# Stick-breaking attention with suffix sums in two float32r passes, one mask matmul and projection quarters between the pairs

## The chip, the cores and the metric

The kernel runs on 1 core of one Trainium2 chip. The metric is the device time in microseconds (us) of one launch, lower is better. The engines are named PE (TensorE, with its weight loads as PEld), DVE (VectorE), ACT (ScalarE), POOL (GpSimd) and SP (SyncE, which issues DMAs).

## What is computed

Two two-layer blocks run one behind the other on a sequence of 256 tokens of width 1024: gated linear attention and an MLP, differential attention and an MLP, retention and a convolutional FFN, stick-breaking attention and a convolutional FFN. The change touches the stick-breaking attention (16 heads of width 64, blocks of 128) and the boundary behind it.

```python
def _stick_breaking(h, w_in, w_out):
    q, k, v = heads(h @ w_in)                 # (B, 16, 256, 64) each
    for i in range(nb):                       # nb = 2 blocks of 128 queries
        def step(carry, xs):                  # key blocks j = i .. 0
            suffix, acc = carry
            z = jnp.einsum('bhqd,bhkd->bhqk', qb, kb) * scale
            mask = s_pos[None, :] < t_pos[:, None]
            log1m = jnp.where(mask, jax.nn.log_sigmoid(-z), 0.0)
            excl = lax.cumsum(log1m, axis=3, reverse=True) - log1m
            log_a = jax.nn.log_sigmoid(z) + excl + suffix[..., None]
            a = jnp.where(mask, jnp.exp(log_a), 0.0)
            acc = acc + jnp.einsum('bhqk,bhkd->bhqd', a, vb)
            suffix = suffix + jnp.sum(log1m, axis=3)
            return (suffix, acc), None
    return o @ w_out                          # then x = x + this
```

With z the masked scores, log1m is minus softplus(z), and the exponent of a weight is z minus the sum of softplus over this key and all later ones that the query sees. The kernel forms that sum over keys as a matmul with a triangular matrix of -1.

## The kernel before

All engines run a program written out by hand, each in its own fixed order, and meet at semaphores. Products with weights are made of three float32r matmuls: high by high, high by low and low by high. A weight chunk of 128 x 2048 is loaded by SP into one of four slots of `raw`; ACT copies its high half to `w_hi` (`hi(c)`), DVE subtracts to give `w_lo` (`lo(c)`), PE multiplies. A slot's `w_hi` may be written again when PE has used it (`used`), its `raw` when `lo` is done.

The attention treats two heads at a time, a pair p = 0..7. The scores of a pair are kept transposed (keys on partitions) in two PSUM banks, `s_bank(p)` and the next, one bank for a head, each with three blocks of 128 columns: key block 0 by query blocks 0 and 1, then key block 1 by query block 1. The steps of a pair are:

- PE `s_scores(p)` (from line 2202): float32 products of `s_k` and `s_q`, then the mask, added by float32r matmuls of the identity with the mask, one for each diagonal block (line 2214).
- ACT `s_log(p)`: ln(1 + exp(-|z|)) in three instructions (lines 958, 960, 962) into `s_b[:, p % 3, 0]`.
- DVE `s_soft(p)` (line 1599): max(z, 0) plus that, the softplus, 768 wide, into `s_b[:, p % 3, 1]`.
- PE `s_weights(p)` (lines 2224, 2226): float32 matmuls of the triangular and the all -1 matrix with these sums, added onto the scores in PSUM. `spm` is waited for.
- ACT `s_exp(p)` (line 967), then PE `s_output(p)` (lines 2237, 2239) with `s_v`, into bank 0 or 1 by turns (for pairs 6 and 7 banks 4 and 5, `so_bank`).
- ACT `s_out(p)` (line 973) copies the output's high half to `h_hi`, DVE `s_lo(p)` (line 1604) subtracts for `h_lo`.

PE's order in the loop is `s_weights(p + 1)`, `s_output(p)`, `s_scores(p + 3)`; ACT's is `s_exp(p)`, `s_out(p - 1)`, `s_log(p + 2)`; DVE's is `s_soft(p + 1)`, `s_lo(p - 1)`. Behind the loop stands the output projection with chunks C_SO to C_SO + 3, which are C_SV + 4 to C_SV + 7 of `hi` and `lo`: two chunks by `h_rows` (line 1650) and two by `last_two` (line 1682), which finishes one output bank after the other. `boundary` is then the passage to the next stage: additions to `x` (line 1117), squares, mean, POOL's power, scaling by DVE (line 1060), transposes on PE (`norm_tile`, line 1695), scaling by ACT (line 632), the split by DVE (lines 1077, 1078), and the first two chunks of the FFN (`first_two`, line 1712).

## Time and profile before

| | us |
|---|---|
| median of 3 runs | 1417.42 |
| lowest and highest | 1415.96, 1417.97 |
| the profiled execution | 1415.18 |
| its span in the trace | 1413.4 |
| PE busy | 1353.4 (96% of the span) |
| DVE busy | 953.1 (67%) |
| ACT busy | 673.1 (48%) |

The span goes from the first to the last instruction of the trace. Busy time is the time in which an engine had an instruction under way. Matmuls overlap: a duration includes the way through the array, so what a matmul costs PE is the distance from its start to the next start. A "line" is a line of the kernel, which can be that of a helper.

### The profile page before, as it was taken

The page shows a single profiled execution, that of the slowest core. Times are in us where ns is not written, and L with a number is a line of the kernel's source. Part 1 is how long each engine was busy: PE and PEld are TensorE (multiplying, and loading weights), DVE is VectorE, ACT ScalarE, POOL GpSimd, SP SyncE. Part 2 cuts the span into 40 slices and gives each one's busy share as a digit, 9 for nine tenths or more (in the row PEclk, how much of TensorE's full clock was granted, in tenths as well). Part 3 has the DMA queues.
Part 4 walks back from the last instruction along what each step waited for, and adds up shares of the span by engine and source line. Part 5 has one row for each costly group of instructions (what it writes and reads, how often), then busy time and mean ns, then how long its engine had stood idle before and what let it go on. Part 6 is the DMA issues. An engine that isn't in the chain of part 4 may idle for free.

```text
span 1413.4 us, 20048 instructions
## 1 busy us (share of the span) xinstructions
PE 1353.4 (96%) x8392; PEld 1189.1 (84%) x8392; DVE 953.1 (67%) x1197; ACT 673.1 (48%) x882; POOL 78.5 (6%) x148
## 2 busy tenths in 40 slices
PE   6899899999999899999899999999999999999997
PEld 1797799998787689998698878999998987999996
DVE  4698787776696876655784445686777534686774
ACT  1553354444556464444533454654545457654542
POOL 1111011110010200000000010000000000000000
PEclk9999999999999999999999999999999999999999
DMA  9786278786392447555265434455553531454530
GB/s 370 276 349 261 89 291 307 289 298 245 137 375 100 160 153 260 218 181 192 105 238 181 176 120 179 149 209 182 188 194 123 216 142 49 160 209 179 187 141 30
DMA packets 46105, 279.41 MB, mean 198 GB/s; under 512 B 5200, under 2 KB 5200, under 8 KB 18880
## 3 DMA queue, kind: packets, MB, share of 16 engines
q1 hardware_dynamic: 33264, 231.57, 44.3%
q0 software_dynamic: 12752, 46.57, 8.8%
q8 instruction: 66, 1.08, 0.3%
q14 instruction: 23, 0.19, 0.0%
HBM read 277.07 MB, written 1.05 MB: 197 GB/s over the span
## 4 chain that ended last, share of the span: by engine, by line
PE 85%; DVE 8%; ACT 3%; issue 2%; DMA 1%; POOL 0%; SPq 0%; POOLq 0%; DVEq 0%; ACTq 0%
PE ps L1650 33%; PE ps L1776 11%; PE ps L1778 11%; PE ps L1777 11%; PE ps L1712 4%; PE ps L1682 3%; DVE w_lo L1010 2%; DMA ada<-in_ada_w 1%; PE ps L1743 1%; PE ps L2010 1%; PE ps L1838 1%; PE ps L1811 1%; DVE acc L1022 1%; DVE h_lo L1078 1%; PE ps L2224 1%
## 5 line engine op out<-in xcount | busy, mean ns | idle before, releaser
L1010 DVE TENSOR_TENSOR w_lo<-raw,w_hi 128x2048 fp32r<-128x2048 f32 x210 | 479.7, 2290 | 178.8 <-ACT w_hi L606 178.2
L606 ACT ACTIVATE w_hi<-raw 128x2048 fp32r<-128x2048 f32 x210 | 400.4, 1911 | 202.9 <-PE ps L1650 154.6
L1776 PE MATMUL ps<-h_hi,w_hi 128*128 128x256 f32 x1344 | 381.8, 284 | 1.9 <-ACT m_r L783 1.9
L1777 PE MATMUL ps<-h_lo,w_hi 128*128 128x256 f32 x1344 | 380.3, 283 | 0.0
L1778 PE MATMUL ps<-h_hi,w_lo 128*128 128x256 f32 x1344 | 380.3, 283 | 0.0
L1776 PEld LDWEIGHTS ps<-h_hi,w_hi 128*128 128x128 f32 x1344 | 256.3, 191 | 4.1 <-ACT m_r L783 2.3
L1777 PEld LDWEIGHTS ps<-h_lo,w_hi 128*128 128x128 f32 x1344 | 256.3, 191 | 1.9 <-issue 0.2
L1778 PEld LDWEIGHTS ps<-h_hi,w_lo 128*128 128x128 f32 x1344 | 256.3, 191 | 0.0
L1561 DVE SCALAR_TENSOR_TENSOR f_cv<-ps,cols,f_cv 128x254 f32<-128x254 f32 (+1 forms) x176 | 76.7, 478 | 70.9 <-ACT f_cv L919 69.3
L1650 PE MATMUL ps<-w_hi,hid_hi 128*128 128x512 f32 x368 | 114.5, 392 | 0.0
L1650 PE MATMUL ps<-w_hi,hid_lo 128*128 128x512 f32 x368 | 114.3, 392 | 0.0
L1650 PE MATMUL ps<-w_lo,hid_hi 128*128 128x512 f32 x368 | 114.1, 391 | 0.0
L1650 PE MATMUL ps<-w_hi,h_hi 128*128 128x512 f32 x328 | 109.4, 397 | 0.4 <-issue 0.4
L1650 PE MATMUL ps<-w_lo,h_hi 128*128 128x512 f32 x328 | 107.1, 390 | 0.0
L1650 PE MATMUL ps<-w_hi,h_lo 128*128 128x512 f32 x328 | 106.9, 389 | 0.0
L1022 DVE SCALAR_TENSOR_TENSOR acc<-ada,csil,acc 128x512 f32<-128x512 f32 x146 | 99.8, 747 | 9.2 <-DMA ada<-in_ada_w 8.9
L919 ACT ACTIVATE f_cv<-ps,cols 128x256 f32<-128x256 f32 x88 | 44.8, 559 | 97.2 <-PE ps L1778 93.6
L1650 PEld LDWEIGHTS ps<-w_lo,hid_hi 128*128 128x128 f32 x368 | 69.1, 188 | 15.1
L1650 PEld LDWEIGHTS ps<-w_hi,hid_lo 128*128 128x128 f32 x368 | 69.1, 188 | 15.0
L1650 PEld LDWEIGHTS ps<-w_hi,hid_hi 128*128 128x128 f32 x368 | 66.1, 188 | 12.0 <-issue 0.5
L1650 PEld LDWEIGHTS ps<-w_hi,h_hi 128*128 128x128 f32 x328 | 61.0, 189 | 14.4 <-issue 2.1
L1650 PEld LDWEIGHTS ps<-w_lo,h_hi 128*128 128x128 f32 x328 | 61.8, 188 | 13.2 <-issue 0.2
(292 smaller groups left out, 1697.6 us busy)
## 6 DMA issues: line engine op xcount, KB each, us to landing
raw<-in_stream SPq DMA_DIRECT2D x210, 1024.0 KB, 4.8
ada<-in_ada_w POOLq DMA_DIRECT2D x80, 512.0 KB, 6.0
ada<-in_ada_w SPq DMA_DIRECT2D x8, 512.0 KB, 12.8
raw<-in_ada_w SPq DMA_DIRECT2D x8, 512.0 KB, 15.6
row<-in_gate_b POOLq DMA_DIRECT2D x3, 512.0 KB, 3.9
x<-in_x SPq DMA_DIRECT2D x1, 1024.0 KB, 9.9
retc<-in_retc POOLq DMA_DIRECT2D x1, 1024.0 KB, 4.9
out<-xn SPq DMA_DIRECT2D x2, 512.0 KB, 2.7
```

What stands on the lines that cost most here:

```text
L606: act.activation(w_hi[:, s, :], raw[:, s, :], ACT.Copy).then_inc(hi_done[s], 1)
L919: last = act.activation(f_cv[:, g % 2, value, f, :], ps[:, 4 + 2 * (g % 2) + value, f * T:(f + 1) * T], ACT.Identity, bias=cols[:, k + 3:k ...
L1010: dve.tensor_tensor(w_lo[:, s, :], raw[:, s, :], w_hi[:, s, :].bitcast(f32), ALU.subtract)\
L1022: dve.scalar_tensor_tensor(acc[:, half], rows, ck, acc[:, half], ALU.mult, ALU.add)\
L1078: dve.tensor_tensor(h_lo[:, *part], h32[:, *part], h_hi[:, *part].bitcast(f32), ALU.subtract)\
L1561: last = dve.scalar_tensor_tensor(v, src, cols[:, k:k + 1], v, ALU.mult, ALU.add)
L1650: return pe.matmul(ps[:, 2 * t + n, :], lhs, w, start=first, stop=stop and k == 1 and p == 2)
L1682: last = pe.matmul(ps[:, 2 * t + n, :], (high, high, low)[p], w, start=False, stop=second == k == 1 and p == 2)
L1712: last = pe.matmul(ps[:, 2 * t + second, 0:T], (high, high, low)[p], w, start=kt == p == 0, stop=kt == KT - 1 and p == 2)
L1776: pe.matmul(out, wh, h_hi[:, kt, :], start=kt == 0, stop=False)
L1777: pe.matmul(out, wh, h_lo[:, kt, :], start=False, stop=False)
L1778: last = pe.matmul(out, wl, h_hi[:, kt, :], start=False, stop=kt == KT - 1)
```

## The change

- Suffix sums: DVE splits the softplus sums into `s_high` (rounded to float32r) and `s_rest` (what is left), and `s_weights` runs the triangular and the -1 matrix over both in float32r. The two matrices are copied, rounded, into `maskr` at the start.
- The blocks in a bank now stand in the order key 0 by query 0, key 1 by query 1, key 0 by query 1, so that both diagonal blocks are neighbours and one mask matmul of 256 columns covers them.
- The output of every pair goes to bank 1. DVE makes both halves (`s_split`); ACT's `s_out` is gone. `s_output(p)` waits until the split of pair p - 1 is done.
- The projection is cut into 16 quarters of six matmuls (`s_project(i, t, n)`: chunk i, token tile t, column half n). Two stand between the pairs, behind p = 3 and p = 5.
- `hi(C_SV + 6)` goes ahead of ACT's last `s_exp`; the order at the boundary is written out anew, with `lo(C_F1)` and `lo(C_F1 + 1)` ahead of the first tile's split.

```diff
-        maskr = sb("maskr", [P, 4 * P], f32r)
+        maskr = sb("maskr", [P, 7 * P], f32r)
+        s_rest = at("s_rest", 6144, [3, 2, 2, 3 * P], f32r)
+        s_high = at("s_high", 10752, [2, 2, 3 * P], f32r)
 ...
+            act.activation(maskr[:, 4 * P:7 * P], shp[:, S_SBM:S_SBM + 3 * P], ACT.Copy).then_inc(mask_done, 1)
 ...
             for p in range(SH_ // 2):
                 s_exp(p)
-                if p >= 1:
-                    s_out(p - 1)
                 if p + 2 < SH_ // 2:
                     s_log(p + 2)
-            s_out(SH_ // 2 - 1)
-            hi(C_SV + 6)
+                if p == 6:
+                    hi(C_SV + 6)
             hi(C_SV + 7)
 ...
             def s_soft(p):
                 dve.wait_ge(sln, p + 1)
-                if p >= 3:
-                    dve.wait_ge(e_mm, p - 2)
-                dve.scalar_tensor_tensor(s_b[:, p % 3, 1, :, :], ..., ALU.max, ALU.add).then_inc(spm, 1)
-
-            def s_lo(p):
+                if p >= 2:
+                    dve.wait_ge(e_mm, p - 1)
+                sums = s_b[:, p % 3, 1, :, :]
+                link(dve.scalar_tensor_tensor(sums, ..., ALU.max, ALU.add))
+                link(dve.tensor_copy(s_high[:, p % 2, :, :], sums))
+                dve.tensor_tensor(s_rest[:, p % 3, 1, :, :], sums, s_high[:, p % 2, :, :].bitcast(f32), ALU.subtract)\
+                    .then_inc(spm, 1)
+
+            def s_split(p):
+                dve.wait_ge(so_mm, p + 1)
+                dve.tensor_copy(h_hi[:, p, :], ps[:, 1, 0:T]).then_inc(so_hi, 1)
                 dve.wait_ge(so_hi, p + 1)
-                dve.tensor_tensor(h_lo[:, p, :], ps[:, so_bank(p), 0:T], h_hi[:, p, :].bitcast(f32), ALU.subtract)\
+                dve.tensor_tensor(h_lo[:, p, :], ps[:, 1, 0:T], h_hi[:, p, :].bitcast(f32), ALU.subtract)\
                     .then_inc(so_lo, 1)
 ...
-                for f, b in half:
-                    for first in (0, T):
-                        last = pe.matmul(ps[:, b, first:first + P], maskr[:, 0:P], maskr[:, 3 * P:4 * P], ...)
+                for f, b in half:
+                    last = pe.matmul(ps[:, b, 0:2 * P], maskr[:, 0:P], maskr[:, 3 * P:5 * P], ...)
 ...
             def s_weights(p):
                 pe.wait_ge(spm, p + 1)
                 for i in range(2):
-                    sums, b = s_b[:, p % 3, 1, i, :], s_bank(p) + i
-                    pe.matmul(ps[:, b, 0:3 * P], shp[:, S_NU:S_NU + P], sums, ...)
-                    last = pe.matmul(ps[:, b, P:2 * P], shp[:, S_NO:S_NO + P], sums[:, 2 * P:3 * P], ...)
+                    b = s_bank(p) + i
+                    for sums in (s_high[:, p % 2, i, :], s_rest[:, p % 3, 1, i, :]):
+                        pe.matmul(ps[:, b, 0:3 * P], maskr[:, 5 * P:6 * P], sums, ...)
+                        last = pe.matmul(ps[:, b, 2 * P:3 * P], maskr[:, 6 * P:7 * P], sums[:, P:2 * P], ...)
                 last.then_inc(e_mm, 1)
 ...
                 pe.wait_ge(sexp, p + 1)
-                if p >= 2:
-                    pe.wait_ge(so_lo, p - 1)
+                if p:
+                    pe.wait_ge(so_lo, p)
 ...
+            def s_project(i, t, n):
+                s = chunk_ready(C_SO + i) if t == n == 0 else (C_SO + i) % NSLOT
+                if t == n == 0:
+                    pe.wait_ge(so_lo, 2 * i + 2)
+                if i == 0 and (t, n) == (0, 1):
+                    pe.wait_ge(so_lo, 8)
+                for k in range(2):
+                    high, low = h_pair(2 * (i // 2))(i % 2, k, t)
+                    for p in range(3):
+                        w = (w_hi, w_lo, w_hi)[p][:, s, k * D + n * 512:k * D + (n + 1) * 512]
+                        last = pe.matmul(ps[:, 2 * t + n, :], (high, high, low)[p], w, ...)
 ...
                 if p + 3 < SH_ // 2:
                     s_scores(p + 3)
-            pe.wait_ge(so_lo, 6)
-            for i in range(2):
-                h_rows(C_SO + i, i, 4)
-            last_two(C_SO + 2, C_SO + 3, h_pair(2), (so_lo, 8), lambda: norm_tile(7, 0))
+                if p in (3, 5):
+                    s_project((p - 3) // 2, 0, 0)
+            s_project(2, 0, 0)
+            s_project(3, 0, 0)
+            for i in range(4):
+                s_project(i, 0, 1)
+            for i in range(4):
+                s_project(i, 1, 0)
+                s_project(i, 1, 1)
+                if i == 2:
+                    norm_tile(7, 0)
```

Two places in the order of the instructions. First PE, from the weights of one pair to the weights of the next. In the kernel before (L2224 and L2226 are the weights, L2237 and L2239 the output, L2208, L2210 and L2214 the scores and masks):

```order
L2224 MATMUL ps<-s_b,shp 128x384 [waits spm]
L2226 MATMUL ps<-s_b,shp 128x128
L2224 MATMUL ps<-s_b,shp 128x384
L2226 MATMUL ps<-s_b,shp 128x128
L2237 MATMUL ps<-s_b,s_v 64x256 [waits so_lo,sexp]
L2237 MATMUL ps<-s_b,s_v 64x256
L2239 MATMUL ps<-s_b,s_v 64x128 x2
L2208 MATMUL ps<-s_q,s_k 128x256 [waits sexp]
L2208 MATMUL ps<-s_q,s_k 128x256
L2210 MATMUL ps<-s_q,s_k 128x128 x2
L2214 MATMUL ps<-maskr 128x128 x4
L2224 MATMUL ps<-s_b,shp 128x384 [waits spm]
```

Weights, output, scores, masks of the pair stand directly behind one another, with nothing of the projection among them. In the changed kernel the same pair, followed by the first quarter of the projection (L2282):

```order
L2250 MATMUL ps<-s_high,maskr 128x384
L2252 MATMUL ps<-s_high,maskr 128x128
L2250 MATMUL ps<-s_rest,maskr 128x384
L2252 MATMUL ps<-s_rest,maskr 128x128
L2263 MATMUL ps<-s_b,s_v 64x256 [waits so_lo,sexp]
L2263 MATMUL ps<-s_b,s_v 64x256
L2266 MATMUL ps<-s_b,s_v 64x128 x2
L2233 MATMUL ps<-s_q,s_k 128x2x128 [waits sexp]
L2233 MATMUL ps<-s_q,s_k 128x2x128
L2236 MATMUL ps<-s_q,s_k 128x128 x2
L2239 MATMUL ps<-maskr 128x256 x2
L2282 MATMUL ps<-w_hi,h_hi 128x512 [waits so_lo,lo_done1,hi_done1]
```

The weights are eight matmuls in two passes instead of four in one, the masks two instead of four, and the quarter stands between the scores and the next pair's weights.

Second DVE, from the last two pairs to the first addition to `x`. Before (L1599 is the softplus sum, L1604 the output's low half, L1010 a chunk's low half, L1117 an addition to `x`):

```order
L1599 SCALAR_TENSOR_TENSOR s_b<-ps,s_b 128x768 [waits e_mm,sln]
L1604 TENSOR_TENSOR h_lo<-ps,h_hi 128x256 [waits so_hi]
L1599 SCALAR_TENSOR_TENSOR s_b<-ps,s_b 128x768 [waits e_mm,sln]
L1604 TENSOR_TENSOR h_lo<-ps,h_hi 128x256 [waits so_hi] x3
L1010 TENSOR_TENSOR w_lo<-raw,w_hi 128x2048 [waits hi_done3]
L1010 TENSOR_TENSOR w_lo<-raw,w_hi 128x2048 [waits hi_done0]
L1010 TENSOR_TENSOR w_lo<-raw,w_hi 128x2048 [waits hi_done1]
L1010 TENSOR_TENSOR w_lo<-raw,w_hi 128x2048 [waits hi_done2]
L1117 TENSOR_TENSOR x<-x,ps 128x512 [waits y_part] x2
```

The last three low halves of outputs follow one another, and all four chunks of this stretch (slots 3, 0, 1 and 2) come ahead of the additions. The same place in the changed kernel (L1604, L1606 and L1607 are the sum and its split, L1612 and L1614 the output's, L1014 a chunk's low half, L1121 an addition):

```order
L1604 SCALAR_TENSOR_TENSOR s_b<-ps,s_b 128x768 [waits e_mm,sln]
L1606 CAST s_high<-s_b 128x768 [waits dve_chain]
L1607 TENSOR_TENSOR s_rest<-s_b,s_high 128x768 [waits dve_chain]
L1612 CAST h_hi<-ps 128x256 [waits so_mm]
L1614 TENSOR_TENSOR h_lo<-ps,h_hi 128x256 [waits so_hi]
L1612 CAST h_hi<-ps 128x256 [waits so_mm]
L1614 TENSOR_TENSOR h_lo<-ps,h_hi 128x256 [waits so_hi]
L1014 TENSOR_TENSOR w_lo<-raw,w_hi 128x2048 [waits hi_done3]
L1612 CAST h_hi<-ps 128x256 [waits so_mm]
L1614 TENSOR_TENSOR h_lo<-ps,h_hi 128x256 [waits so_hi]
L1014 TENSOR_TENSOR w_lo<-raw,w_hi 128x2048 [waits hi_done0]
L1121 TENSOR_TENSOR x<-x,ps 128x512 [waits y_part] x2
```

Each sum has become three instructions, each output's low half two, and the low half of slot 3 (chunk C_SO + 2) stands between the last two splits. The low halves of slots 1 and 2 (C_F1 and C_F1 + 1) have moved behind the first two additions.

## Rows read from the trace of the kernel before

**Rows 1.** Busy time by stretch: from:to, length, PE, PEld, DVE, ACT, POOL, PEclk, DMA, GB/s.

```profile
1151.49:1190.74 39.25, 38.00 (x249) 27.78 (x248) 10.63 (x15) 30.48 (x43) 0.00 (x0) 1.00 0.07 27
1190.74:1213.50 22.76, 22.76 (x106) 18.82 (x105) 13.18 (x13) 11.56 (x18) 0.55 (x1) 1.00 0.49 185
1240.00:1260.00 20.00, 20.00 (x134) 18.46 (x134) 18.57 (x27) 11.43 (x12) 0.00 (x0) 1.00 0.72 263
```

**Rows 2.** Timeline of PE, one pair: start, length, engine, line, operation, count, idle before.

```profile
1167.01 0.86 PE L2224 MATMUL ps<-s_b,shp 128*128 128x384 f32 x2
...
1168.89 0.65 PE L2237 MATMUL ps<-s_b,s_v 128*64 128x256 f32 x4
...
1169.69 0.70 PE L2208 MATMUL ps<-s_q,s_k 64*128 64x256 f32 x4
...
1170.55 0.66 PE L2214 MATMUL ps<-maskr 128*128 128x128 f32 x4
1171.05 0.86 PE L2224 MATMUL ps<-s_b,shp 128*128 128x384 f32 x2
```

**Rows 3.** Timeline of ACT, the same pair: abs (L958) and exp of the weights (L967).

```profile
1167.21 0.81 ACT L958 ACTIVATE s_b<-ps 128x768 f32<-128x768 f32 x1 [0.41 <-PE ps L2214]
...
1169.77 0.79 ACT L967 ACTIVATE s_b<-ps 128x768 f32<-128x768 f32 x1
...
1171.24 0.81 ACT L958 ACTIVATE s_b<-ps 128x768 f32<-128x768 f32 x1 [0.41 <-PE ps L2214]
```

**Rows 4.** Timeline of DVE, the sum of the same pair.

```profile
1169.90 0.96 DVE L1599 SCALAR_TENSOR_TENSOR s_b<-ps,s_b 128x768 f32<-128x768 f32 x1 [2.64 <-ACT s_b L962]
```

**Rows 5.** Timeline of PE: end of the value projection, last weights, start of the output projection.

```profile
1159.80 0.81 PE L2224 MATMUL ps<-s_b,shp 128*128 128x384 f32 x2
...
1187.04 0.91 PE L2224 MATMUL ps<-s_b,shp 128*128 128x384 f32 x2 [1.15 <-DVE s_b L1599]
...
1190.74 0.73 PE L1650 MATMUL ps<-w_hi,h_hi 128*128 128x512 f32 x2
```

**Rows 6.** Timeline of PE in the differential attention: its masks, then the next product.

```profile
437.76 0.51 PE L2037 MATMUL ps<-maskr 128*128 128x256 f32 x2
438.10 0.40 PE L2010 MATMUL ps<-w_hi,h_hi 128*128 128x512 f32 x1
```

**Rows 7.** Groups of DVE by form: line, operation, shapes, count, busy, mean ns, idle before.

```profile
L1077 DVE CAST h_hi<-h 128x256 fp32r<-128x256 f32 x56 | 16.3, 291 | 19.9 <-ACT h L632 19.9
...
L1579 DVE TENSOR_TENSOR hid_lo<-f_p,hid_hi 128x512 fp32r<-128x512 f32 x22 | 15.2, 692 | 0.8
...
L1578 DVE CAST hid_hi<-f_p 128x512 fp32r<-128x512 f32 x22 | 9.4, 427 | 1.9 <-PE ps L1650 1.2
...
L1272 DVE COPY g_st<-ps 128x256 f32<-128x256 f32 x4 | 1.7, 420 | 0.9 <-PE ps L1913 0.9
```

**Rows 8.** The page's costliest groups: the low and the high half of a chunk.

```profile
L1010 DVE TENSOR_TENSOR w_lo<-raw,w_hi 128x2048 fp32r<-128x2048 f32 x210 | 479.7, 2290 | 178.8 <-ACT w_hi L606 178.2
L606 ACT ACTIVATE w_hi<-raw 128x2048 fp32r<-128x2048 f32 x210 | 400.4, 1911 | 202.9 <-PE ps L1650 154.6
```

**Rows 9.** Timeline of DVE: the fourth addition to x behind the projection.

```profile
1214.59 0.68 DVE L1117 TENSOR_TENSOR x<-x,ps 128x512 f32<-128x512 f32 x1
```

**Rows 10.** Timeline of PE: the second tile's transposes and the product behind them.

```profile
1217.88 1.03 PE L1695 MATMUL ps<-shp,xn 128*128 128x128 f32 x8
1218.67 0.36 PE L1712 MATMUL ps<-w_hi,h_hi 128*128 128x256 f32 x1
```

**Rows 11.** Busy time by stretch, as in rows 1, where PE worked little.

```profile
458.00:464.00 6.00, 2.99 (x25) 2.43 (x23) 5.89 (x14) 4.05 (x23) 2.89 (x7) 1.00 0.11 15
464.00:470.00 6.00, 3.60 (x20) 3.41 (x21) 5.56 (x20) 1.06 (x6) 1.94 (x4) 0.69 0.40 162
470.00:476.00 6.00, 4.91 (x29) 4.42 (x28) 2.66 (x8) 4.06 (x19) 2.69 (x6) 0.74 0.00 0
680.00:700.00 20.00, 13.82 (x78) 11.25 (x76) 15.58 (x31) 9.92 (x26) 2.32 (x3) 1.00 0.16 58
```

More of the change, by code:

```diff
@@ L718, in _ @@
             act.activation(maskr[:, 0:P], ident, ACT.Copy)
-            act.activation(maskr[:, P:4 * P], shp[:, S_CAUS:S_CAUS + 3 * P], ACT.Copy).then_inc(mask_done, 1)
+            act.activation(maskr[:, P:4 * P], shp[:, S_CAUS:S_CAUS + 3 * P], ACT.Copy)
+            act.activation(maskr[:, 4 * P:7 * P], shp[:, S_SBM:S_SBM + 3 * P], ACT.Copy).then_inc(mask_done, 1)
             act.wait_ge(ada_pe, KT)
@@ L968, in s_exp @@
                     .then_inc(sexp, 1)
-            def s_out(p):
-                act.wait_ge(so_mm, p + 1)
-                act.activation(h_hi[:, p, :], ps[:, so_bank(p), 0:T], ACT.Copy).then_inc(so_hi, 1)
             s_log(0)
@@ L979, in _ @@
                 s_exp(p)
-                if p >= 1:
-                    s_out(p - 1)
                 if p + 2 < SH_ // 2:
                     s_log(p + 2)
-            s_out(SH_ // 2 - 1)
-            hi(C_SV + 6)
+                if p == 6:
+                    hi(C_SV + 6)
             hi(C_SV + 7)
+            scale_col = lambda kt: cols[:, COL_FFN + KT + kt:COL_FFN + KT + kt + 1]
+            square(X_SB, 0)
+            square(X_SB, 1)
             hi(C_F1)
             hi(C_F1 + 1)
-            boundary(7, X_SB, TR_N7, lambda kt: cols[:, COL_FFN + KT + kt:COL_FFN + KT + kt + 1], None, C_F1, 5)
+            norm_tile(TR_N7, 0, scale_col, None)
+            square(X_SB, 2)
+            square(X_SB, 3)
+            hi(C_F1 + 2)
+            evacuate(5, 0, (fc_mm, 11), ACT.Copy)
+            norm_tile(TR_N7, 1, scale_col, None)
+            evacuate(5, 1, (fc_mm, 12), ACT.Copy)
+            hi(C_F1 + 3)
+            evacuate(5, 2, multiplied(C_F1), ACT.Copy)
+            evacuate(5, 3, multiplied(C_F1 + 1), ACT.Copy)
             ffn(1, C_F1)
@@ L1611, in _ @@
                 if p >= 1:
-                    s_lo(p - 1)
-            s_lo(SH_ // 2 - 1)
+                    s_split(p - 1)
             lo(C_SV + 6)
+            s_split(SH_ // 2 - 1)
             lo(C_SV + 7)
-            for c in range(C_SO, C_SO + 2):
-                lo(c + 4)
-            boundary(add_plain, Y_SOUT, 7, TR_N7, C_F1)
+            add_plain(Y_SOUT, 0)
+            add_plain(Y_SOUT, 1)
+            norm_mean(7, 0)
+            scale_tile(7, 0)
+            lo(C_F1)
+            lo(C_F1 + 1)
+            split_tile(TR_N7, 0, 0, 4)
+            add_plain(Y_SOUT, 2)
+            add_plain(Y_SOUT, 3)
+            norm_mean(7, 1)
+            scale_tile(7, 1)
+            split_tile(TR_N7, 1, 0, 4)
+            lo(C_F1 + 2)
+            lo(C_F1 + 3)
             ffn(1, C_F1)
```

36 lines of the change are left out of this document (22 added, 14 removed).

## The prediction

> **What bounds the kernel now.** I read busy time by stretch first [rows 1], then the instructions of one pair of heads in order of time on PE, ACT and DVE [rows 2 to 4]. The change touches one stage, from the first scores at 1151.49 us to the end of the output projection at 1213.5 us: 62 of 1413.4 us. In it PE is busy 38.00 of 39.25 us over the eight pairs and all 22.76 us of the projection [rows 1], so PE sets the pace. The reader should see in [rows 2] that a pair costs 4.04 us of PE: weights 1167.01 to 1168.89 = 1.88, output to 1169.69 = 0.80, scores with masks to 1171.05 = 1.36 (masks alone 1170.55 to 1171.05 = 0.50).
>
> A second limit lies close behind. The scores of a pair must pass ACT (abs, exp, ln), DVE (the softplus sum) and come back to PE for the weights, and two pairs are in flight. Around that loop: abs starts 1167.21, DVE's sum ends 1170.86, PE could start at 1170.91: 3.70 us [rows 3, 4]. Then PE's 1.88 + 0.80 + 1.36, then 0.20 from the scores' end at 1171.05 to the next abs at 1171.24. Together 7.94 us for two pairs, against 8.06 of PE work. The slack is 0.12 us for two pairs. That is the number on which this forecast hangs: whatever shortens PE by more than it gives nothing, and whatever lengthens ACT or DVE inside the loop is paid.
>
> **The masks.** Four 128-column float32r matmuls become two of 256 columns. The first form takes 0.50 us [rows 2], the second stands in the earlier attention at 437.76 to 438.10 = 0.34 [rows 6]. Scores fall from 1.36 to 1.20. The strided output of the scores has no row. Its ends are 0 and, if each half paid a start of its own, 0.10 a pair. I take 0.
>
> **The weights.** Per pair, four matmuls of plain float32 (two of 384 and two of 128 columns, each two records) become eight of float32r. The projection's 96 matmuls of 512 columns, six to a quarter, take (22.76 - 0.79) / 96 = 0.229 us each [rows 1, 10]; 0.79 is a tile's transposes (1217.88 to 1218.67). At the full clock a column is 1/2.4 ns, so 384 columns take 0.229 - 0.053 = 0.175. A 128-column one follows from the two mask forms: 4x - 2 x 0.122 = 0.50 - 0.34, x = 0.10. Weights then cost 4 x 0.175 + 4 x 0.10 + 0.12 for the change of type = 1.22 us, against 1.88. Ends: 1.06 (128 columns at the column rate) and 1.35 (0.125 each, 0.15 for the change). I take 1.22, which has the nearest row.
> The Trainium skill (TensorE: Matmul & The Clock Gate, section Back-to-back issue gap) gives an isolated gap of N/2.4 + 2.5 ns, 56 ns at 128 columns. By it the weights would cost about 1.04 and the end would come near 1419.8; the mask rows speak for 0.10 and the row decides.
>
> **PE in sum.** 0.16 + 0.66 = 0.82 us less per pair, 6.6 us over eight. PE needs 3.22 us a pair.
>
> **The split of the sums (DVE).** To feed float32r, DVE casts the 768-wide sum to s_high and subtracts it to give s_rest, both before the weights may start. A cast takes 0.291 at 256 and 0.427 at 512 [rows 7], so 0.565 at 768. A subtraction takes 0.692 at 512 and 2.290 at 2048 [rows 7, 8], so 0.958. Each waits some 0.04 for the instruction before it. That adds 1.60 us inside the loop. Ends: 1.45, and 2.0 if the cast ran at the subtraction's rate.
>
> **The loop after.** 3.70 + 1.60 + 1.22 + 0.80 + 1.20 + 0.20 = 8.72 us for two pairs, 4.36 a pair, where it was 4.03. The 6.6 us taken from PE become idle time, and each pair is 0.33 us longer than before. The quarters of the projection go into that idle time (4.36 - 3.22 = 1.14), but one quarter is 1.37.
>
> **The copy of the output.** The h_hi copy moves from ACT to DVE, where a 256-wide copy from PSUM takes 0.420 [rows 7]. With the subtraction a split is 0.89. All outputs now share bank 1, so output(p) waits for split(p-1). Within the loop DVE has that time free. At the end it has not: output(7) stands right behind output(6), with no work between.
>
> **The walk.** Two shorter scores bring the value projection's end from 1159.80 [rows 5] to 1159.48. Weights(0) and scores(2) end at 1161.90, abs at 1162.10, and weights(2) start at 1167.40 (before: 1167.01). The odd chain: scores(3) end 1165.12, ACT is free at 1165.35, weights(3) at 1170.75 with 0.1 for a split ahead on DVE. Weights(4) at 1176.12; PE is through with scores(6) at 1179.34 and then does the first quarter until 1180.71, while weights(5) could have started at 1179.47. So that quarter pushes the odd chain by 1.24. Weights(6) at 1184.84, the second quarter (1186.86 to 1188.23) is hidden, weights(7) at 1180.71 + 3.42 + 5.30 = 1189.43. Before it was 1187.04 [rows 5]. Output(6) ends 1191.45, split(6) is done at 1192.5, output(7) ends 1193.35. Before: 1190.74 [rows 5]. ACT's high half of C_SO+2, moved ahead of exp(7), fits in ACT's wait and costs nothing.
>
> **The projection.** Two quarters are done, 14 are left. The low half of chunk C_SO+2 stands on DVE behind split(6): 1192.5 + 2.29 = 1194.8 [rows 8]. PE waits 1.5 us for it. Then split(7), and the low half of C_SO+3 until 1197.9: PE waits 1.7 us again. Before, both chunks were long ready. The fourth quarter ends at 1199.3, twelve more 16.4, the transposes 0.79: end at 1216.5, against 1213.5. The two waits, 3.2 us, eat the 2.7 us that the quarters between the pairs had won. **+3.0 us.**
>
> **The next boundary.** Before, DVE's fourth addition to x starts at 1214.59, 1.05 us behind the projection's end, and the second tile's transposes start 3.29 later at 1217.88 [rows 9, 10]. Now both additions of tile 1 stand behind the low halves of C_F1 and C_F1+1 and the splits of tile 0. PE frees C_F1+1's slot 2.7 us before the transposes of tile 0; high half 1.91 and low half 2.29 [rows 8] then end 1.8 us before the projection's end, the splits 0.9 behind it, and the fourth addition starts 1.5 behind it. PE waits some 0.3 us longer. **+0.3 us.** ffn(1) behind it is bound by PE (20.00 of 20.00, [rows 1]), so the shift goes through to the end. The wider mask copy at the kernel's start is one ACT instruction where ACT has nothing to do: 0.
>
> **Sum.** +3.3 us: the profiled span of 1413.4 becomes 1416.7, its own time of 1415.18 becomes 1418.5. The median shown is 1417.42, 2.2 us above that execution, so 1417.42 + 3.3 = **1420.7 us**, 0.23% slower. About 0.2%, 2.8 us, is what a measurement can tell from no change, and my sum lies close to that line. Moving one term at a time through the walk: weights at 1.06 takes off 0.8, at 1.35 adds 0.65; the split at its high end adds 1.2; a strided output at 0.10 adds 0.5. Terms together span about +1.3 to +5.5.
>
> **Rivals.**
> *A, as summed*: 1420.7, own range 1420.2 to 1422.5. Chance 0.45.
> *B, the cheap ends*: weights near 1.06, the PSUM copy at the SBUF cast's 0.29, and a shorter split. The same mechanism gives +1.5 to +2.7, near 1419.5, no measurable change. For it speaks that the 128-column cost rests on a difference of two rows. 0.33.
> *C, PE's clock falls*. From 1188.2 to 1198 PE works in my walk some 4.4 of 9.8 us. In the earlier attention PE was busy 2.99 of 6 us from 458 to 464, and the granted clock was 0.69 and 0.74 over the two stretches behind it, so it stood at 1.2 GHz for about 6.8 us [rows 11]. In a stretch bound by PE that costs about half, 3.4 us: 1424.1. Against it: from 680 to 700 us PE was busy 13.82 of 20 us and the clock stayed 1.00 [rows 11], and no single wait in my walk exceeds 1.8 us. 0.13.
> The Trainium skill (TensorE: Matmul & The Clock Gate, section What's actually happening) says that the throttled clock is the default and activity releases it; both rows fit that, and neither tells how thin 1188 to 1198 may be.
> *D, the other side: the loop does not bind*. If ACT already held each pair's scores when it got free, pairs would be spaced by what each engine does: DVE 2.56 + 0.81 = 3.4, ACT 3.3, PE 3.22 and the quarters. Weights(7) would start near 1186.3, 3.1 us sooner than in my walk: 1417.6, not slower. It decides as soon as scores(p+3) end before exp(p+1) does; in [rows 2, 3] they end after it with today's order, which the change keeps. 0.05. With B's costs on top, or without the two waits for low halves, it is faster by more than 0.2% (about 1414.5): 0.04.
>
> Slower 0.58, same 0.38, faster 0.04. The range, 1417.5 to 1424.3, takes in A, B, most of D and half of C.
>
> **What would show it.** In the changed kernel's trace: weights blocks of about 1.2 us spaced by some 4.4 us, PE idle 1.1 us before most of them, released by DVE's s_rest; weights(7) near 1189.4; two PE waits of 1.5 and 1.7 us for w_lo at the third and fourth quarter; the end of the projection near 1216.5. Wrong if pairs are 3.4 us apart, if the cast takes 0.96, or if the granted clock drops near 1195.

## The result and the profile after

| | before | after |
|---|---|---|
| median | 1416.7 us (5 runs, 1415.5 to 1417.97) | 1422.27 us (5 runs, 1421.14 to 1424.66) |
| ratio | | 1.0042, 95% interval [1.0029, 1.0055] |
| the profiled execution, its span | 1415.18, 1413.4 | 1421.14, 1419.4 |
| PE, DVE, ACT busy | 1353.4, 953.1, 673.1 | 1352.8, 967.8, 671.5 |

The changed kernel is 0.4% slower. PE's busy time is the same to 0.6 us although its matmuls got cheaper. Stages ahead of this one take a different time in each execution (the first scores start at 1151.49 us before, at 1150.65 after, and between 1151.95 and 1153.78 in the profiled executions of the experiments), so I compare the stretch from the first scores to the second tile's transposes of the next boundary. It was 1217.88 - 1151.49 = 66.39 us [rows 10] and is 1223.81 - 1150.65 = 73.16 us: **6.77 us longer**.

First PE's time line of the changed kernel (start, duration, engine, line, operation; in brackets the idle time ahead and its releaser), which answers to [rows 2] and [rows 6]. L2250 and L2252 are the weights, L2263 and L2266 the output, L2233 and L2236 the scores, L2239 the mask:

```profile
1160.99 0.34 PE L2250 MATMUL ps<-s_high,maskr 128*128 128x384 f32 x1
1161.16 0.22 PE L2252 MATMUL ps<-s_high,maskr 128*128 128x128 f32 x1
1161.23 0.39 PE L2250 MATMUL ps<-s_rest,maskr 128*128 128x384 f32 x1
1161.45 0.22 PE L2252 MATMUL ps<-s_rest,maskr 128*128 128x128 f32 x1
1161.51 0.39 PE L2250 MATMUL ps<-s_high,maskr 128*128 128x384 f32 x1
...
1162.18 0.65 PE L2263 MATMUL ps<-s_b,s_v 128*64 128x256 f32 x4
...
1162.98 0.70 PE L2233 MATMUL ps<-s_q,s_k 64*128 64x256 f32 x4
...
1163.83 0.50 PE L2239 MATMUL ps<-maskr 128*128 128x256 f32 x2
1166.48 0.44 PE L2250 MATMUL ps<-s_high,maskr 128*128 128x384 f32 x1 [2.15 <-DVE s_rest L1607]
```

Weights take 1162.18 - 1160.99 = 1.19 us (1.88 before), output 0.80, scores with masks about 1.19 (1.36 before). Then PE waits 2.15 us for DVE's `s_rest`. DVE's time line shows what it waits for, beside [rows 4]:

```profile
1163.88 0.96 DVE L1604 SCALAR_TENSOR_TENSOR s_b<-ps,s_b 128x768 f32<-128x768 f32 x1 [4.04 <-ACT s_b L961]
1164.87 0.56 DVE L1606 CAST s_high<-s_b 128x768 fp32r<-128x768 f32 x1
1165.46 0.96 DVE L1607 TENSOR_TENSOR s_rest<-s_b,s_high 128x768 fp32r<-128x768 f32 x1
1166.34 0.42 DVE L1612 CAST h_hi<-ps 128x256 fp32r<-128x256 f32 x1
```

The cast and the subtraction stand between the sum and the weights, 1.58 us. The rest is in three stretches of the changed kernel (length, then busy time and instructions of PE, PEld, DVE, ACT, POOL, granted clock, DMA share, GB/s): the pairs, the passage to the projection, and the projection, beside [rows 1]:

```profile
1150.65:1191.50 40.85, 35.02 (x231) 27.65 (x232) 24.27 (x36) 29.52 (x36) 0.00 (x0) 0.96 0.07 26
1191.50:1199.00 7.50, 4.43 (x24) 2.82 (x24) 6.01 (x6) 2.61 (x2) 0.00 (x0) 0.82 0.34 107
1199.00:1221.00 22.00, 22.00 (x100) 18.28 (x100) 10.22 (x16) 7.66 (x15) 0.55 (x1) 0.91 0.38 143
```

Before, PE was busy 38.00 of 39.25 us in the pairs and all of the projection, at clock 1.00. Now it idles 5.8 us in the pairs, 3.1 in the passage, and the granted clock is 0.96, 0.82 and 0.91. Its waits from 1191 us on:

```profile
1193.39 0.65 PE L2263 MATMUL ps<-s_b,s_v 128*64 128x256 f32 x4 [1.08 <-DVE h_lo L1614]
1195.54 0.47 PE L2282 MATMUL ps<-w_hi,h_hi 128*128 128x512 f32 x1 [1.28 <-issue]
1198.53 0.77 PE L2282 MATMUL ps<-w_hi,h_hi 128*128 128x512 f32 x1 [0.70 <-issue]
...
1223.81 1.09 PE L1716 MATMUL ps<-shp,xn 128*128 128x128 f32 x8 [0.34 <-DVE xn L1064]
```

Output(7) waits for the split of output(6) (the shared bank 1), and the third and fourth projection quarter start when DVE's low halves are through: "issue" names no releaser, but DVE's `w_lo` ends at 1193.16 + 2.28 = 1195.44 and 1196.15 + 2.28 = 1198.43, 0.1 us ahead of each. The clock in half-microsecond windows (length, PE busy, clock, DMA share, GB/s):

```profile
1175.50:1176.00 0.50, 0.50 (x5) 0.77 0.00 0
1176.00:1176.50 0.50, 0.50 (x5) 0.50 0.00 0
...
1178.50:1179.00 0.50, 0.50 (x4) 0.50 0.00 0
1179.00:1179.50 0.50, 0.50 (x6) 0.82 0.00 0
...
1196.00:1196.50 0.50, 0.50 (x4) 0.74 0.85 98
1196.50:1197.00 0.50, 0.50 (x3) 0.50 0.83 131
...
1202.50:1203.00 0.50, 0.50 (x3) 0.50 0.06 17
1203.00:1203.50 0.50, 0.50 (x4) 0.93 0.00 0
```

PE ran at 1.2 GHz from about 1175.8 to 1179.2 us (3.4 us) and from 1196.2 to 1203.0 us (6.8 us). The first fall comes behind a wait of 2.08 us ahead of weights(4), the second inside the passage, in which PE had been busy 2.34 of the 4.70 us from 1191.5 us on.

This execution is the fastest of the five. Each execution lists the mean granted clock of its whole run, and the slower it was, the lower that clock: 0.988 at 1421.14 us, 0.987 at 1421.50, 0.984 at 1422.27, 0.983 at 1424.50 and 0.982 at 1424.66. So the falls seem to be longer or more frequent in the others, of which there is no trace.

### The profile page after: what moved, and what is told of

It is laid out like the page before. It is cut to its first block, busy times and chain, and to the rows that moved or that the text cites. A ratio compares the mean times of both kernels' runs of the same rounds, so it can differ in the third digit from the quotient of the medians.

```text
span 1419.4 us, 20035 instructions
## 1 busy us (share of the span) xinstructions
PE 1352.8 (95%) x8376; PEld 1189.8 (84%) x8376; DVE 967.8 (68%) x1221; ACT 671.5 (47%) x875; POOL 78.5 (6%) x148
## 4 chain that ended last, share of the span: by engine, by line
PE 83%; DVE 9%; ACT 3%; issue 2%; DMA 1%; POOL 0%; SPq 0%; POOLq 0%; DVEq 0%; ACTq 0%
PE ps L1671 32%; PE ps L1797 11%; PE ps L1799 11%; PE ps L1798 11%; PE ps L1733 4%; PE ps L1703 2%; DVE w_lo L1014 2%; DMA ada<-in_ada_w 1%; PE ps L2282 1%; PE ps L1764 1%; PE ps L2031 1%; PE ps L1859 1%; PE ps L1832 1%; DVE acc L1026 1%; ACT w_hi L604 1%
## 5 line engine op out<-in xcount | busy, mean ns | idle before, releaser
L1014 DVE TENSOR_TENSOR w_lo<-raw,w_hi 128x2048 fp32r<-128x2048 f32 x210 | 479.8, 2290 | 175.1 <-ACT w_hi L604 174.5
L1671 PE MATMUL ps<-w_hi,h_hi 128*128 128x512 f32 x312 | 104.3, 397 | 0.3 <-issue 0.3
L1671 PE MATMUL ps<-w_lo,h_hi 128*128 128x512 f32 x312 | 102.4, 391 | 0.0
L1671 PE MATMUL ps<-w_hi,h_lo 128*128 128x512 f32 x312 | 102.0, 389 | 0.0
L1671 PEld LDWEIGHTS ps<-w_lo,h_hi 128*128 128x128 f32 x312 | 58.9, 189 | 12.6 <-issue 0.2
L1671 PEld LDWEIGHTS ps<-w_hi,h_hi 128*128 128x128 f32 x312 | 58.0, 189 | 13.6 <-issue 2.0
```

The source lines that it names most:

```text
L1014: dve.tensor_tensor(w_lo[:, s, :], raw[:, s, :], w_hi[:, s, :].bitcast(f32), ALU.subtract)\
L1671: return pe.matmul(ps[:, 2 * t + n, :], lhs, w, start=first, stop=stop and k == 1 and p == 2)
```

## The experiments

The theory: the loop of two pairs is bound by its latency (the time that a pair needs to go round PE, ACT and DVE), so cheaper PE work gives nothing and DVE's 1.6 us are paid; the quarters' gain is lost to waits for low halves at the end; the idle PE then loses its clock. The rivals are told with each run. All medians and ratios stand in this table, with the stretch from the first scores to the second transposes in each kernel's one profiled execution, the start of weights(7) behind the first scores, and the time that PE stood at 1.2 GHz in the stretch.

| kernel | ratio to before, interval | stretch | weights(7) | at 1.2 GHz |
|---|---|---|---|---|
| before | | 66.39 | 35.55 | 0 |
| after | 1.0042 [1.0029, 1.0055] | 73.16 | 39.50 | 3.4 + 6.8 |
| e1_fill | 1.0019 [1.0010, 1.0029] | 69.50 | 37.95 | 0 |
| e2_float32_sums | 1.0011 [1.0001, 1.0020] | 68.00 | 35.95 | 0 |
| e3_low_half_early | 1.0028 [1.0016, 1.0039] | 71.52 | 41.04 | 3.4 + 3.4 |
| e4_masks_alone | 0.9990 [0.9980, 0.9999] | 65.19 | 34.35 | 0 |
| e5_scores_ahead | 1.0019 [1.0009, 1.0028] | 69.40 | 35.70 | 6.8 |
| e6_masks_and_passes | 1.0036 [1.0022, 1.0049] | 70.18 | 38.45 | 3.4 + 6.8 |
| e7_ahead_before_tail | 0.9994 [0.9985, 1.0002] | 64.51 | 34.31 | 0 |
| e8_high_early | 0.9975 [0.9965, 0.9984] | 62.78 | 32.17 | 0 |
| e9_two_quarters | 0.9963 [0.9949, 0.9977] | 60.35 | 32.98 | 0 |
| e10_boundary_order | 0.9983 [0.9974, 0.9992] | 63.98 | 32.98 | 3.4 |
| e11_own_banks | 1.0047 [1.0032, 1.0063] | 71.42 | 39.48 | 3.4 + 3.4 |
| e12_banks_and_halves | 1.0019 [1.0009, 1.0029] | 68.48 | 40.65 | 6.8 |

**The clock.** The changed kernel, with matmuls on banks that nobody reads in the places where PE waits:

```diff
+            def fill(n, bank):
+                for _ in range(n):
+                    pe.matmul(ps[:, bank, 0:T], maskr[:, 0:P], maskr[:, P:3 * P], start=True, stop=True)
...
+                if p in (0, 2):
+                    fill(14, 0)
...
             s_project(2, 0, 0)
+            fill(8, 2)
```

(Seven more stand ahead of output(7), five behind the second quarter and eight ahead of the third. The edit adds 56 matmuls in all; the 42 of the expectation is a miscount.)

> The changed kernel plus 42 matmuls of 256 columns into a PSUM bank that nobody reads, put where PE stood idle in the changed kernel's trace (14 ahead of weights(2), 14 ahead of weights(4), 5 ahead of weights(7), 7 ahead of output(7), 8 ahead of each of the third and fourth quarters less the one already counted; each group shorter than the idle time). They compute nothing. Theory 1 (the fall of PE's clock is about 3.6 of the 6 us that the change costs): the granted clock stays 1.00 from the first scores to the end of the projection, that stretch takes 65.0 us instead of 68.6, and the kernel is 3 to 4 us faster than the changed one: 1418.5, ratio to before near 1.0015. Theory 2 (the pairs and the waits cost it all, the clock's fall lies in time in which PE would have waited anyway): clock 1.00 but the stretch stays at 68 us and the time at 1422 or above.

Median 1419.13 us. The clock stayed at 1.00 over the pairs, the passage and the projection:

```profile
1152.48:1193.33 40.85, 39.01 (x276) 31.94 (x276) 24.85 (x38) 31.05 (x38) 0.00 (x0) 1.00 0.07 26
1193.33:1200.00 6.67, 6.06 (x38) 4.84 (x37) 5.36 (x5) 1.11 (x1) 0.00 (x0) 1.00 0.47 160
1200.00:1221.00 21.00, 21.00 (x112) 18.03 (x112) 10.74 (x17) 9.49 (x19) 0.97 (x2) 1.00 0.38 150
```

The stretch is 69.50 us: the two falls cost 3.66 us in the profiled execution, 1.55 ahead of weights(7) (39.50 - 37.95) and 2.11 behind it. The medians come out near it: 1422.27 - 1419.13 = 3.1.

**The passes.** One plain float32 pass in place of the two, with the rest of the change kept:

```diff
-                link(dve.scalar_tensor_tensor(sums, ...))
-                link(dve.tensor_copy(s_high[:, p % 2, :, :], sums))
-                dve.tensor_tensor(s_rest[...], sums, s_high[...].bitcast(f32), ALU.subtract).then_inc(spm, 1)
+                dve.scalar_tensor_tensor(s_b[:, p % 3, 1, :, :], ...).then_inc(spm, 1)
```

> The changed kernel with the suffix sums in one float32 pass again (no s_high, no s_rest); block order, one mask matmul, bank 1, quarters and boundary as changed. Theory 1 (DVE's split lies inside the loop of two pairs and lengthens it): weights blocks are 1.88 us and pairs 3.9 us apart, PE is hardly idle between pairs, the clock stays 1.00 there; weights(7) start 36.9 us behind the first scores (35.55 before the change, 39.5 in the changed kernel; two quarters of 1.37 are in it); the two waits for low halves remain. 1416.5 to 1418. Theory 2 (the two passes are worth their PE time and something else in the change costs, such as the shared bank or the split on DVE): as slow as the changed kernel or slower, 1422 to 1425, pairs 4.3 us or more apart.

Stretch 68.00 us, median 1417.76, clock 1.00. Weights(7) start at 35.95, 0.95 us sooner than expected. At the full clock the two passes therefore cost 69.50 - 68.00 = 1.5 us in this surrounding, and the rest of the change is 1.6 us behind the kernel before.

**The masks.** The kernel before with the block order and the one mask matmul, nothing else:

```diff
-                    for first in (0, T):
-                        last = pe.matmul(ps[:, b, first:first + P], maskr[:, 0:P], maskr[:, 3 * P:4 * P],
+                    last = pe.matmul(ps[:, b, 0:2 * P], maskr[:, 0:P], maskr[:, 3 * P:5 * P],
```

> The kernel before the change with one part of it alone: the new order of the blocks and one mask matmul of 256 columns for both diagonal blocks. Theory 1 (PE bound with a slack of 0.12 us for two pairs): a block of scores takes 1.20 instead of 1.36 us, pairs are 3.89 us apart instead of 4.03, the projection starts 1.2 to 1.5 us sooner: 1415.4, ratio 0.9991. If the strided output of the scores costs something, a block of scores takes 1.3 us or more and the gain is under 0.6 us.

Stretch 65.19, 1.20 us shorter than before; the strided output costs nothing that shows. So the part of the change beside masks and passes (one output bank, quarters, waits at the end, boundary) costs 68.00 - 65.19 = 2.8 us. It adds up from rows: two quarters leave the end (-2.74), weights(7) start 35.95 - 34.35 = 1.60 later, output(7) comes 0.88 later behind them, the third and fourth quarter wait 1.28 + 1.37, the boundary 0.1: together 2.5. The other 0.3 us I can't put down to a row.

**The low halves.** The changed kernel with the high and low half of chunk C_SO + 2 one to two pairs earlier:

```diff
+                if p == 4:
+                    hi(C_SV + 6)
                 if p + 2 < SH_ // 2:
                     s_log(p + 2)
-                if p == 6:
-                    hi(C_SV + 6)
...
                     s_split(p - 1)
+                if p == 4:
+                    lo(C_SV + 6)
```

> The changed kernel with the high half of chunk C_SO+2 made by ACT behind exp(4) and its low half by DVE behind the split of pair 3, where both engines stood idle for over 2 us. Theory 1 (PE's two waits at the end come from low halves that stand between the last splits): the wait of 1.28 us ahead of the third quarter goes, the fourth quarter's low half is ready about 2.2 us earlier, and the projection's end comes 2 to 3 us sooner if the clock's fall moves with it, at least 1.3 if it does not: 1419.5 to 1421. Theory 2 (PE has to wait for the output's last split anyway): less than 0.7 us.

The wait ahead of the third quarter is gone; the fourth waits 1.63 us, since its low half still stands behind split(7). But in this execution the clock fell twice in the pairs, behind 2.15-us waits, and not at the end:

```profile
1168.50:1169.00 0.50, 0.50 (x3) 0.50 0.00 0
...
1178.50:1179.00 0.50, 0.50 (x3) 0.66 0.00 0
```

With different falls in the two traces the 1.6 us between them can't be put down to the low half alone. Behind weights(7) the clock held both here and in e1_fill, so that part can be compared: 71.52 - 41.04 = 30.48 us here and 69.50 - 37.95 = 31.55 there. The early low half is worth 1.1 us, a little less than the 1.3 expected, since 1.28 us of waiting went and the fourth quarter's wait grew from 1.37 to 1.63.

**The shared bank.** Outputs 6 and 7 in banks 4 and 5:

```diff
+        def so_bank(p):
+            return p - 2 if p >= 6 else 1
...
-                if p:
+                if 0 < p < 6:
                     pe.wait_ge(so_lo, p)
```

> The changed kernel with outputs 6 and 7 in banks 4 and 5 and not in bank 1, so that output(7) does not wait for DVE's split of output(6). Theory: the 1.08 us wait ahead of output(7) goes, and the wait ahead of the third quarter grows by as much, since DVE's order (split, low half, split, low half) is untouched and the low half comes last: first scores to second transposes 73.1 us as in the changed kernel, 1422 us, ratio 1.004. Rival (the shared bank costs its wait): 1.1 us less, 1421.1, ratio 1.0033.

The wait ahead of output(7) is gone and stands, whole, ahead of the third quarter:

```profile
1193.70 0.65 PE L2267 MATMUL ps<-s_b,s_v 128*64 128x256 f32 x4
...
1196.83 0.47 PE L2286 MATMUL ps<-w_hi,h_hi 128*128 128x512 f32 x1 [2.26 <-issue]
...
1199.82 0.77 PE L2286 MATMUL ps<-w_hi,h_hi 128*128 128x512 f32 x1 [0.48 <-issue]
```

Third quarter at 1196.83 - 1151.95 = 44.88 us behind the first scores, in the changed kernel 1195.54 - 1150.65 = 44.89. The bank costs nothing, because DVE's order ahead of the quarters is the later limit. The trace is 1.74 us shorter all the same: its second fall lasted 3.4 us and not 6.8. The median says no such thing (1421.74 us, 1.0047), which shows how far one trace can be trusted where falls differ.

**Bank and both halves.** As the last one, with both chunks' halves made in the idle time between the pairs:

```diff
+                if p == 4:
+                    hi(C_SV + 6)
...
+                if p == 5:
+                    hi(C_SV + 7)
...
+                if p == 4:
+                    lo(C_SV + 6)
+                if p == 6:
+                    lo(C_SV + 7)
```

> As e11_own_banks, and ACT and DVE make the high and low halves of both C_SO+2 and C_SO+3 in their idle time between the pairs (behind log(6) and log(7); behind the splits of pairs 3 and 5). Theory: no wait is left between weights(7) and the transposes of the first tile, 1.0 + 1.3 + 0.7 us go, and with them the thin stretch behind which the clock fell at the end; the falls behind the 2-us waits in the pairs stay. First scores to second transposes 66.6 us at full clock, 68.1 to 70 with falls in the pairs: 1417 to 1419 us, ratio 1.0005 to 1.002. Rival (the end is limited otherwise): 71.5 or more, ratio 1.003.

No wait is left between weights(7) and the transposes of tile 0, and there is no fall at the end; one of 6.8 us remains in the pairs, behind the wait ahead of weights(2). Stretch 68.48, median 1418.73: 2.94 us less than with own banks alone, for 2.26 + 0.48 = 2.74 us of waits taken away at about as much time at 1.2 GHz.

**Latency or work.** The changed kernel, with the scores one turn earlier. Each engine does the same work.

```diff
                 s_output(p)
-                if p + 3 < SH_ // 2:
-                    s_scores(p + 3)
+                if p == 0:
+                    s_scores(3)
+                if p + 4 < SH_ // 2:
+                    s_scores(p + 4)
```

> The changed kernel with one edit: PE issues the scores of a pair one turn earlier (scores(p+4) behind output(p), where it was scores(p+3)); same instructions, same work. Theory (the latency of the loop sets the pace, because ACT must wait for scores that PE issues too late): ACT then always has the next pair's scores, and the loop of two pairs is weights to exp 1.29, exp 0.69, abs/exp/ln 2.65, the sum, cast and subtraction 2.68 = 7.31 us, 3.66 a pair, where it is 8.72. weights(7) starts 3.3 us sooner than in a run at full clock, at about 34.6 us behind the first scores (39.5 in the changed kernel), the waits ahead of the weights are under 1 us each, and the clock stays at 1.00 in the pairs. First scores to second transposes: 66.2 us if the clock also holds at the end (1416.0 us, ratio 0.9999), 68.3 if it falls there again (1418.1, 1.0013). Rival (PE or DVE work sets the pace, 4.3 us a pair): spacing stays near 4.3, ratio 1.002 to 1.004.

Weights(2), (4) and (6) start at 1169.17, 1176.74 and 1184.30: 7.57 us for two pairs, where the changed kernel has 8.77 (1166.48 to 1175.25). So order and latency set the pace there, and not an engine's work. The spacing decides this; the ratio, 1.0019, lies near the range that the rival had. The waits ahead of the weights are short:

```profile
PE ps L2250 <- DVE s_rest L1607: 2.7, 4, 1.0
PE ps L2282 <- issue: 2.0, 2, 1.3
PE ps L2263 <- DVE h_lo L1614: 1.1, 1, 1.1
```

(us in total, times, the longest.) My 7.31 was too low in two terms: from weights to exp it is 1.40 and not 1.29, from exp to abs 0.87 and not 0.69. Weights(7) start at 35.70, not 34.6. The end of the stage is the changed kernel's, and there the clock fell again, for 6.8 us:

```profile
1192.00:1194.00 2.00, 0.87 (x8) 1.00 0.00 0
1194.00:1196.00 2.00, 1.55 (x5) 0.80 0.23 37
1196.00:1198.00 2.00, 1.28 (x3) 0.50 0.94 385
```

From weights(7) to the second transposes it takes 33.70 us, in the changed kernel 33.66, in e1_fill 31.55.

**The passes in the old surroundings.** Before, with the masks and the two passes:

```diff
-                    sums, b = s_b[:, p % 3, 1, i, :], s_bank(p) + i
+                    b = s_bank(p) + i
+                    for sums in (s_high[:, p % 2, i, :], s_rest[:, p % 3, 1, i, :]):
```

> The kernel before with the one mask matmul and the two float32r passes, and nothing else of the change: outputs alternate between two banks, ACT makes their high half, the projection and the boundary stand behind the pairs as before. Theory: the loop of two pairs is as in the changed kernel, 8.7 us, so the weights start in turns of two 8.7 us apart, weights(7) near 36.6 us behind the first scores (34.35 with the masks alone), and the shorter last weights give 0.7 back: first scores to second transposes 66.8 us (65.19 with the masks alone, 66.39 before), 1416.6 us, ratio 1.0003, if the clock holds. If the 2-us waits ahead of every other weights bring it down once more, as in the changed kernel, 1.5 to 3.7 us are on top: up to 1420.3, 1.003. Rival (the passes cost nothing by themselves, the rest of the change does): 1414.3 to 1415, ratio 0.999.

Weights(2) to weights(4) 8.77 us again. The clock fell behind weights(4) and weights(6), for 3.4 and 6.8 us, and the stretch is 70.18: 5.0 us behind the masks alone. The median, 1420.58 us, lies just above the 1420.3 that I had allowed for falls. The passes, through the loop and the clock (as long at 1.2 GHz as in the changed kernel), make 5.0 of the 8.0 us by which the changed kernel's stretch is behind that of the masks alone; the projection's order isn't needed for them.

**Scores ahead, old end of the stage**, both halves of an output on DVE:

```diff
-                act.activation(h_hi[:, p, :], ps[:, so_bank(p), 0:T], ACT.Copy).then_inc(so_hi, 1)
+                dve.tensor_copy(h_hi[:, p, :], ps[:, so_bank(p), 0:T]).then_inc(so_hi, 1)
```

> The kernel of e6_masks_and_passes with the scores one turn earlier and both halves of the output split on DVE (copy and subtraction, as in the changed kernel). Theory: 3.66 us a pair, limited by ACT and DVE in turn; weights(7) at about 33.7 us behind the first scores (35.55 before, 34.35 with masks alone), last weights 1.2 us; first scores to second transposes 63.9 us, 1413.7 us, ratio 0.9983, clock 1.00. Rival (what cost 2.8 us in the changed kernel beside the passes is the split on DVE, not the order of the projection): 1416 or more, ratio 1.000.

Stretch 64.51, not 63.9, since two pairs take 7.56 here too. The median is 1415.11 us (0.9994), so no difference to before that these runs show, and 1.4 us above my forecast. It lies between the theory's time and the rival's. 5.7 us of e6's stretch are gone with the order and the copy on DVE, which no run separates, and the clock held, although PE waited 2.04 us ahead of weights(6) and 1.20 ahead of weights(7) a pair later.

**High parts first.** PE multiplies both heads' high parts while DVE still subtracts:

```diff
-                link(dve.tensor_copy(s_high[:, p % 2, :, :], sums))
+                dve.tensor_copy(s_high[:, p % 2, :, :], sums).then_inc(s_hi, 1)
+                dve.wait_ge(s_hi, p + 1)
...
-                pe.wait_ge(spm, p + 1)
-                for i in range(2):
+                for n in range(2):
+                    pe.wait_ge(spm if n else s_hi, p + 1)
+                    for i in range(2):
```

> The kernel of e7_ahead_before_tail, in which PE multiplies both heads' high parts while DVE still makes the low ones (a semaphore of its own behind the cast). Theory: 0.6 us leave the loop of two pairs (6.7 us), but DVE's own work of 3.45 us a pair (sum, cast, subtraction, split) then sets the pace: weights(7) at about 32.5 us behind the first scores, first scores to second transposes 62.7 us, 1412.5 us, ratio 0.9974. Rival (changing between high and low of the two heads costs as much as it hides, or DVE already sets the pace): as e7_ahead_before_tail, 0.998.

Stretch 62.78 for 62.7, median 1412.9 us. It beats the kernel before by 0.25%. The pace seems to be not DVE's, as I had said, but ACT's, which has nearly no gap left (from 1168 to 1182 us ACT was busy 13.31 of 14 us, DVE 12.88, PE 12.59): weights(2) to weights(4) are 6.99 us, and ACT's exponentials of pairs 3 to 5 stand as follows, 6.99 us from the first to the third:

```profile
1172.91 0.79 ACT L971 ACTIVATE s_b<-ps 128x768 f32<-128x768 f32 x1
...
1176.47 0.81 ACT L971 ACTIVATE s_b<-ps 128x768 f32<-128x768 f32 x1
...
1179.90 0.79 ACT L971 ACTIVATE s_b<-ps 128x768 f32<-128x768 f32 x1
```

**Two quarters that nothing waits for.**

```diff
-            return p - 2 if p >= 6 else p % 2
+            return p - 2 if p >= 6 else 1 if p >= 4 else p % 2
...
+                if p in (4, 5):
+                    s_project(p - 4, 0, 0)
```

> The kernel of e8_high_early with two of the sixteen projection quarters moved between the pairs, behind output(4) and output(5), where PE waits about 1.0 us for s_high; outputs 4 and 5 share bank 1 so that bank 0 is free for them, outputs 6 and 7 keep banks of their own, and the rest of the projection and the boundary stay as before. Theory (a quarter between the pairs wins what it fills, if nothing behind it comes to wait for a low half or a bank): 2.74 us of projection leave the end, the last weights start some 1.0 us later: first scores to second transposes 61.1 us (62.78 in e8_high_early, 66.39 before), 1411.2 us, ratio 0.9963, clock 1.00. Rival (the quarters are what costs in the changed kernel): 62.8 or more, ratio 0.9975 or above.

Stretch 60.35 us, **1410.1 us median, 0.9963**: faster than both kernels. The quarters are worth 62.78 - 60.35 = 2.4 us here: weights(7) start only 0.8 later, 2.74 leave the end, and the last weights take 1.19 us and not 1.71, because `s_rest` is ready in time. The quarters fill nearly all that PE had left to wait ahead of the weights:

```profile
1152.42:1189.00 36.58, 35.68 (x248) 28.19 (x248) 25.62 (x40) 30.21 (x37) 0.00 (x0) 1.00 0.08 29
```

**The boundary's order.** The last kernel with the changed kernel's order on ACT and DVE behind the projection:

```diff
-            for c in range(C_SO, C_SO + 2):
-                lo(c + 4)
-            boundary(add_plain, Y_SOUT, 7, TR_N7, C_F1)
+            add_plain(Y_SOUT, 0)
...
+            scale_tile(7, 0)
+            lo(C_F1)
+            lo(C_F1 + 1)
+            split_tile(TR_N7, 0, 0, 4)
+            add_plain(Y_SOUT, 2)
```

> The kernel of e9_two_quarters with the changed kernel's order at the next boundary (DVE: both additions of tile 1 behind the low halves of C_F1, C_F1+1 and the splits of tile 0). Theory, as forecast: PE starts the second tile's transposes about 0.3 us later: 61.4 us against 61.1, ratio about 0.0002 above e9_two_quarters. Rival (the boundary order is a good part of the 2.8 us by which the changed kernel without its passes is behind the masks alone): 1 us or more, ratio 0.001 above.

The rival is right: the stretch is 63.98, 3.6 us longer, and the ratio 0.0020 higher. PE's and DVE's time lines:

```profile
1206.94 4.49 DVE L1018 TENSOR_TENSOR w_lo<-raw,w_hi 128x2048 fp32r<-128x2048 f32 x2 [0.23 <-ACT w_hi L609]
...
1212.24 0.36 PE L1738 MATMUL ps<-w_hi,h_hi 128*128 128x256 f32 x1 [2.29 <-DVE h_lo L1086]
```

Both low halves of the FFN's first chunks stand ahead of the split of tile 0, while in e9_two_quarters ACT and DVE had made them from 1192.83 on, as soon as their slots came free. PE waits 2.29 us of the 3.6, and behind that the clock fell for 3.4 us. The changed kernel doesn't pay this, because it projects tile 0 to the end before it starts tile 1: between the second addition and the transposes of tile 0 it has 1207.77 to 1215.74 = 8.0 us for these halves, this kernel 1203.65 to 1207.54 = 3.9. The order at the boundary and the order of the projection belong together.

## Why the prediction was right, and where it was not

It said 1420.7 us (1417.5 to 1424.3), slower. Measured were 1422.27, slower. The mechanism forecast, a loop bound by latency and an end whose waits eat what the quarters win, is what the runs show; the clock, a second cost of nearly the same size, was missing from the sum. The steps:

- **Durations.** Weights 1.22 a pair: 1.19. Scores 1.20: 1.19. Cast 0.565 and subtraction 0.958: 0.56 and 0.96. Copy of the output 0.420: 0.42. By the formula that the Trainium skill gives for an isolated gap (TensorE: Matmul & The Clock Gate, section Back-to-back issue gap) a matmul of 384 and one of 128 columns would take 0.22 us together, an estimate. From start to start of the second such group the trace has 1161.51 - 1161.23 = 0.28, and the measurement decides.
- **The loop of two pairs**, 8.72 us: 8.77 (1166.48 to 1175.25), and 8.78 for the odd pairs (1160.99 to 1169.77). That it is latency and not work was shown by e5_scores_ahead.
- **The walk**, behind the first scores: weights(2) 15.91, measured 15.83; weights(4) 24.63, 24.60; weights(7) 37.94, 39.50 in the changed kernel and 37.95 with the clock held in e1_fill. The first quarter pushed the odd chain as said.
- **The waits at the end.** 1.5 and 1.7 us: 1.28 and 1.37 at the full clock (e2_float32_sums), 1.28 and 0.70 in the changed kernel, whose slower third quarter used up part of the second wait. The waits and the quarters' gain cancel, as said; e12_banks_and_halves took the waits away and e9_two_quarters showed the gain without them, 2.4 us.
- **The boundary**, +0.3: PE waits 0.34 us ahead of the second transposes; they start 4.69 us behind the start of the projection's last matmul (1219.12 to 1223.81), before it was 4.56 (1213.32 to 1217.88): 0.1 us later.
- **The sum** of all that, +3.3 us: e1_fill's stretch is 69.50 - 66.39 = 3.1 us longer than before. Its projection ends at 1217.52, 65.0 us behind its first scores, as in the forecast (1216.5 - 1151.49).
- **The clock is the step that failed.** It was rival C, with a chance of 0.13, placed at the end only, and a drop near 1195 us was one of the forecast's own signs of being wrong: it came at 1196.2. It fell there, and once in the pairs as well: 3.66 us in the profiled execution, 3.1 by the medians. Against it I held that no single wait in my walk was over 1.8 us. That was wrong by the walk itself, in which scores(3) end at 1165.12 and weights(2) start at 1167.40: I had spread the idle time evenly, 1.14 us a pair, where it comes as nothing ahead of weights(3) and (5), 2.15 us ahead of weights(2) and 2.08 ahead of weights(4). The case that came true is A and C together, +3.1 and +3.7 in the traces. That the forecast lies only 1.6 us below the median is in part luck: the median rose by 1422.27 - 1416.7 = 5.6 us and not by 3.3, but the forecast started from 1417.42, which three executions had given, and five gave 1416.7.

What stays open is which idle time brings the clock down. In the traces of this case it fell behind single waits of 1.81 to 2.29 us (after, e3, e6, e10, e11, e12) and in passages with several waits (after, e5). It held through a wait of 2.04 us in e7_ahead_before_tail, through a passage with 6.28 of 10 us busy in e2_float32_sums, and through the 2.15 us ahead of weights(2) in the changed kernel and in e6, where in e3 and e12 it fell behind the same wait. Ten executions of e5_scores_ahead spread from 1415.37 to 1420.09 us; that this is the fall coming and going is not shown, since only the execution of 1420.09 us has a trace.
